# Reordered small loads in layer 1: constants ahead of weight panels, the router's loads and the norm's squares inside the merge stage

## The reference, cut to what matters

```python
y_gdn = gdn_output(o_x, x_z, gdn_norm_g[l])          # rms norm per head, times gdn_norm_g, times silu(z)
y_sgu = sgu_mixer(x_u, x_v, lat_chunks, sgu_ln_g[l], sgu_ln_b[l], sgu_w[l], sgu_b[l])
x = x + mod_x[:, 2][:, None, :] * merge_branches(y_gdn, y_sgu, x_gates, w_branch_a[l], w_branch_b[l], w_out[l])
hx = modulate(rms_norm(x, norm_ffn_g[l]), mod_x[:, 3], mod_x[:, 4])
x = x + mod_x[:, 5][:, None, :] * hier_moe(hx, router_group_w[l], router_group_b[l], router_expert_w[l], ...)
```

## Time and profile before

| | us |
|---|---|
| median of 3 runs | 1783.42 (1783.27 to 1786.96) |
| the profiled execution | 1784.11 |
| its span in the profile | 1782.4 |
| TensorE busy | 1526.9 (86%) |
| VectorE busy | 810.9 (45%) |

### The profile page before, as it was taken

One profiled execution on the slowest core, in us unless ns is written; L12 is line 12 of the kernel. 1 busy time (PEld: TensorE's weight loads), 2 busy tenths in 40 slices (PEclk: granted clock), 3 DMA queues, 4 the chain that ended last, 5 costly groups with the idle time before them and its releaser, 6 DMA issues. The chain is left out here.

```text
span 1782.4 us, 19489 instructions
## 1 busy us (share of the span) xinstructions
PE 1526.9 (86%) x7553; PEld 896.7 (50%) x7553; DVE 810.9 (45%) x1512; ACT 371.3 (21%) x700; POOL 191.1 (11%) x280
## 2 busy tenths in 40 slices
PE   4999968779879989475789876999889899999977
PEld 2877766578634434242334333444444447656563
DVE  2344548444456376541211114266573315675553
ACT  3221245111101100110000001000350224642230
POOL 0000016500000000002000000000250001213330
PEclk9899979777989999677989997999999999999998
DMA  9331002220577766569999993433501222121120
GB/s 347 100 94 48 1 1 58 78 83 10 177 269 270 259 246 231 209 242 410 414 364 368 394 382 123 150 133 106 154 3 69 94 72 71 48 95 47 49 72 24
DMA packets 132298, 283.60 MB, mean 159 GB/s; under 512 B 28744, under 2 KB 39272, under 8 KB 126955
## 3 DMA queue, kind: packets, MB, share of 16 engines
q1 hardware_dynamic: 128608, 266.65, 41.6%
q0 software_dynamic: 3600, 15.73, 2.2%
HBM read 312.77 MB, written 4.19 MB: 178 GB/s over the span
## 5 line engine op out<-in xcount | busy, mean ns | idle before, releaser
L1383 PE MATMUL ps<-ring,hTx 128*128 128x512 f32 x256 | 113.4, 600 | 3.4 <-PEq L176 1.8
L2678 PE MATMUL ps<-hT,ring 128*128 128x512 f32 x256 | 111.8, 593 | 3.1 <-PEq L2585 2.8
L325 DVE SCALAR_TENSOR_TENSOR ada_acc<-ring,cact,ada_acc 128x512 f32<-128x512 f32 x154 | 104.1, 744 | 0.5
L629 PE MATMUL ps<-hTx,ring 128*128 128x256 f32 x384 | 91.0, 392 | 5.3 <-PEq L176 5.3
L2313 PE MATMUL ps<-hT,ring 128*128 128x512 f32 x208 | 90.4, 592 | 0.0
L629 PEld LDWEIGHTS ps<-hTx,ring 128*128 128x128 f32 x384 | 74.7, 197 | 19.6 <-issue 8.0
L1383 PEld LDWEIGHTS ps<-ring,hTx 128*128 128x128 f32 x256 | 48.7, 193 | 62.8 <-issue 60.4
L2678 PEld LDWEIGHTS ps<-hT,ring 128*128 128x128 f32 x256 | 47.9, 190 | 61.0 <-issue 61.0
L1899 PE MATMUL ps<-ring,hTx 128*32 128x512 f32 x384 | 54.0, 713 | 26.8 <-DMA ring<-in_expert_w 26.8
L720 DVE SCALAR_TENSOR_TENSOR conv<-xpad,taps,conv 128x512 f32<-128x512 f32 (+1 forms) x96 | 63.6, 663 | 3.4
L2313 PEld LDWEIGHTS ps<-hT,ring 128*128 128x128 f32 x208 | 39.5, 190 | 48.5 <-issue 48.3
(11 more groups left out here) (526 smaller groups left out, 2723.7 us busy)
## 6 DMA issues: line engine op xcount, KB each, us to landing
ring<-in_expert_w SPq DMA_DIRECT2D x24, 2048.0 KB, 14.7
far<-in_expert_w SPq DMA_DIRECT2D x24, 2048.0 KB, 18.6
ring<-in_w_in SPq DMA_DIRECT2D x16, 2048.0 KB, 12.8
ring<-in_ada_w SPq DMA_DIRECT2D x12, 2048.0 KB, 9.6
ring<-in_w_ada SPq DMA_DIRECT2D x12, 2048.0 KB, 8.9
ring<-in_w_in_c SPq DMA_DIRECT2D x10, 2048.0 KB, 8.4
ring<-in_expert_w POOLq DMA_DIRECT2D x32, 512.0 KB
far<-in_expert_w POOLq DMA_DIRECT2D x32, 512.0 KB
```

Of the source, the lines that this page charges most:

```text
L325: ins = dve.scalar_tensor_tensor(out=part, in0=slot[:, kt], scalar=c[:, kt:kt + 1], in1=part, op0=ALU.mult, op1=ALU.add)
L629: ins = pe.matmul(ps[:, j % BANKS, s * L:(s + 1) * L], slot[:, kt, (j % 4) * P:(j % 4 + 1) * P], (hTc, hTx)[s][:, kt], start=(kt == 0), st ...
L1383: ins = pe.matmul(ps[:, 2 + i % BANKS], hTx[:, kt, t * P:(t + 1) * P], stream.slot(n)[:, kt], start=(kt == 0), stop=(kt == KT - 1))
L2678: ins = pe.matmul(bank, slot[:, kt, j % 4 * P:(j % 4 + 1) * P], hT[:, kt], **edge)
```

## The change

1. In the u/v/gate block SP issues the five small loads `spw`, `spb_row`, two `ln_rows` and `gn_row` before the two panels rather than behind them. The four bias rows `mods` stay behind.
2. SP issues the seven loads that the router needs (`grow`, two parts of `wr`, two of `br`, `slots`, `slot_col`) in the merge block, behind `xs`, `mod_x` and `mod_c`, and ahead of the block's panels. SP waits at the block's end until they have landed; TensorE and VectorE no longer wait for them in the route block. Their tiles move to a scope that lives longer.
3. The two squares of `xs` move from the head of the route block to the end of the merge block on ScalarE; their elementwise output goes to `merged`, which is no longer used by then.
4. In the merge block VectorE waits for the bias rows behind the second `dot`, ahead of the first `put`, rather than ahead of everything.

```diff
@@ u/v/gate block
                     def _(sp):
-                        stream.issue(sp, uvg[1] + 1)
                         sp.dma_start(spw[:, :, :], w["sgu_w"][0].rearrange("g p q -> p g q")).then_inc(loaded, 16)
                         sp.dma_start(spb_row[:, :], w["sgu_b"][0]).then_inc(loaded, 16)
                         sp.dma_start(ln_rows[:, 0], row_bcast(w["sgu_ln_g"][0])).then_inc(loaded, 16)
                         sp.dma_start(ln_rows[:, 1], row_bcast(w["sgu_ln_b"][0])).then_inc(loaded, 16)
                         sp.dma_start(gn_row[:, :], row_bcast(w["gdn_norm_g"][0])).then_inc(loaded, 16)
+                        stream.issue(sp, uvg[1] + 1)
@@ merge block
+                        sp.dma_start(grow[:, :], row_bcast(w["norm_ffn_g"][0])).then_inc(route_loaded, 16)
+                        sp.dma_start(wr[:, :, 0:GROUPS], pkt(w["router_group_w"][0])).then_inc(route_loaded, 16)
+                        sp.dma_start(wr[:, :, GROUPS:], pkt(w["router_expert_w"][0])).then_inc(route_loaded, 16)
+                        sp.dma_start(br[:, 0:GROUPS], row_bcast(w["router_group_b"][0])).then_inc(route_loaded, 16)
+                        sp.dma_start(br[:, GROUPS:], row_bcast(w["router_expert_b"][0])).then_inc(route_loaded, 16)
+                        at, n = parts["slots"]
+                        sp.dma_start(slots[:, :], const_dram[:, at:at + n]).then_inc(route_loaded, 16)
+                        at, n = parts["slot_col"]
+                        sp.dma_start(slot_col[:, :], const_dram[:, at:at + n]).then_inc(route_loaded, 16)
                         stream.issue(sp, ab_in[0])
+                        sp.wait_ge(route_loaded, 112)
...
                     def _(dve):
-                        dve.wait_ge(bias_loaded, 32)
                         for i in range(4 * TT):
                             if i % TT == 0 and i // TT < 3:
                                 dot(dve, i // TT)
+                                if i == TT:
+                                    dve.wait_ge(bias_loaded, 32)
                                 if i:
                                     put(dve, i // TT - 1)
...
+                        for t in range(TT):
+                            act.wait_ge(added, TT + t + 1)
+                            act.activation(merged[:, t], xs[:, t], ACT.Square, accum_out=stat[:, t:t + 1])
@@ route block
-                            sp.dma_start(grow[:, :], row_bcast(w["norm_ffn_g"][0])).then_inc(loaded, 16)
...
-                            for t in range(TT):
-                                if t:
-                                    act.wait_ge(squares, t)
-                                act.activation(sqr[:, :], xs[:, t], ACT.Square, accum_out=stat[:, t:t + 1]).then_inc(squares, 1)
                             act.wait_ge(steps, 1)
...
-                            pe.wait_ge(loaded, 112)
...
-                            dve.wait_ge(squares, TT)
                             dve.tensor_scalar(stat[:, 2:4], stat[:, 0:2], 1.0 / D, EPS, ALU.mult, ALU.add).then_inc(steps, 1)
-                            dve.wait_ge(loaded, 112)
                             dve.scalar_tensor_tensor(out=gm[:, :], in0=mods[:, 2], scalar=1.0, in1=grow[:, :], op0=ALU.add, op1=ALU.mult).then_inc(steps, 1)
```

More of the change, by code:

```diff
@@ L1302, in build @@
             mods = sb(first, "mods", [P, 4, D])
+            grow = sb(first, "grow", [P, D])
+            wr = sb(first, "wr", [P, KT, ROUTER])
+            br = sb(first, "br", [P, ROUTER])
+            slots = sb(first, "slots", [P, SLOTS])
+            slot_col = sb(first, "slot_col", [P, SLOTS // P])
             branches = first.enter_context(ExitStack())
@@ L1489, in build @@
                     ssem(n) for n in ("proj", "gated", "summed", "turned", "moved", "outed", "scaled", "added"))
-                bias_loaded, x_loaded = ssem("bias_loaded"), ssem("x_loaded")
+                bias_loaded, x_loaded, route_loaded = (ssem(n) for n in ("bias_loaded", "x_loaded", "route_loaded"))
                 BANKS = 6
@@ L1628, in build @@
                 with ExitStack() as scope:
-                    grow = sb(scope, "grow", [P, D])
                     gm = sb(scope, "gm2", [P, D])
@@ L1650, in build @@
                     ssem = stage_sems(scope, "route_")
-                    loaded, squares, steps, std, turned, moved, routed, ge_done, e2_done, chain, ordered, chosen_done, ranked, gated, slotted, rowed = (
-                        ssem(n) for n in ("loaded", "squares", "steps", "std", "turned", "moved", "routed", "ge_done", "e2_done", "chain", "ordered", "chosen_done",
+                    steps, std, turned, moved, routed, ge_done, e2_done, chain, ordered, chosen_done, ranked, gated, slotted, rowed = (
+                        ssem(n) for n in ("steps", "std", "turned", "moved", "routed", "ge_done", "e2_done", "chain", "ordered", "chosen_done",
                                           "ranked", "gated", "slotted", "rowed"))
```

13 lines of the change are left out of this document (removed).

## The result

| | before, beside it | changed |
|---|---|---|
| median, us | 1785.18 (1783.27 to 1787.12, 8 runs) | 1774.15 (1770.67 to 1781.40, 8 runs) |
| ratio | | 0.9943, 95% interval 0.9924 to 0.9962 |
| span of the profiled execution | 1782.4 | 1769.9 |

The ratio is a gain of 10.2 us (6.8 to 13.6). It is faster, as forecast, but 1774.15 is 6.7 us above the forecast of 1767.4 and outside its range of 1763.0 to 1771.5. Six microseconds less came than the 16.0 forecast. Of the changed kernel's eight runs four took 1770.7 to 1772.0 us and four 1776.3 to 1781.4, and the median stands between the two groups; the profiled execution, 1772.01, is of the lower one.

What follows compares the result with a forecast made beforehand. TensorE was taken as the bound from 512 to 611.7, with winnable waits before and behind it; gains of 4.0 + 2.0 + 10.0 = 16.0 us gave a span-based 1768.1 and a median of 1767.4 us, range 1763.0 to 1771.5.

Steps and rivals of the forecast that it cites:

- part 2: Merge block: `w_branch_b` issued earlier, its landing set by the queue with seven loads added, 647.4 instead of 649.37; gain 2.0 us.
- starting value of 1783.4: Whole kernel: the profiled execution's 1784.11 us less 0.7 for the median, from which the gains were taken.
- Faster at all: Whole kernel: the claim that the change is faster by over 0.2%; chance 0.95.
- Part 1, gain 4.0: Head of the u/v/gate block: `gn_row` lands early, the third `uvg` panel ends at 519.3 instead of 523.35; gain 4.0 us.
- Part 3, gain 10.0: Head of the route block: first product for `h2` 1.8 us after the block's start instead of 11.8; gain 10.0 us.
- the rival: Merge: `wr` stalls SP and `w_branch_b` lands late; ends slower only if it lands at 667 or later; chance 0.02.
- rival of dearer loads: Merge and u/v/gate: small loads cost more than their share, merge loses 2.5 us; 1770.5 to 1774 us; chance 0.2.
- Clock: Waits for second `uvg` panel and `w_branch_b` end at the lower clock, costing 2.5 us each; rival, clock stays up: chance 0.13.

Runs made afterwards that it cites:

- e11_squares_back: e3_loads_last with the two squares of `xs` back at the head of the route block; 1771.42 us, ratio 0.9901.
- e2_nohead: The changed kernel with the five small loads of the u/v/gate block back in their old order behind the panels; 1777.33 us, ratio 0.9950.
- e5_few_pieces: The changed kernel with `wr` loaded as contiguous rows, 128 pieces per part instead of 1024, and copied into place by GpSimd; 1772.75 us, ratio 0.9915.
- e6_wait_only: The kernel before with only VectorE's wait for the merge's bias rows moved behind the second `dot`; 1774.50 us, ratio 0.9935.
- e12_no_part4: The changed kernel with the wait for the bias rows left at the front of the merge's first `dot`; 1776.15 us, ratio 0.9937.
- e3_loads_last: The changed kernel with the seven router loads issued behind the merge's last panel; 1763.01 us, ratio 0.9868.
- e8_best: e3_loads_last with only `gn_row` ahead of two `uvg` panels, the third ahead of `ln_rows` and `mods`, and the `mods` wait behind the second `dot`; 1761.13 us.
- e4_best: e3_loads_last with `gn_row`, `spw` and `spb_row` ahead of two `uvg` panels, the third panel ahead of `ln_rows` and `mods`; 1766.35 us, ratio 0.9873.
- e10_best_again: The same kernel as e8_best, run again with more runs; 1760.11 us, ratio 0.9837.
- e16_wr_last: The changed kernel with both parts of `wr` and `br` behind the merge's last panel, `grow`, `slots` and `slot_col` left ahead; 1767.83 us, ratio 0.9886.
- e1_head: The kernel before with only the five small u/v/gate loads moved ahead of the two panels; 1781.79 us, ratio 0.9970.
- e7_after_again: The changed kernel, unaltered, measured once more; 1772.99 us, ratio 0.9923.

## Why the prediction was wrong in size and right in sign

The step of the mechanism that failed is the one of part 2 that took SP's stall as harmless and let the queue alone set when `w_branch_b` lands. In size a second step weighs more: that all outside the three blocks stays at nothing, from a starting value of 1783.4. Of the 6.7 us above the forecast 1.8 lie in that starting value (before's median was 1785.18 beside the changed kernel) and 5.0 in the gain, 11.0 us between the medians instead of 16.0; of these, 1.2 are part 2's and most of the rest lies outside the blocks.

- **Faster at all** (0.95): right. The third `uvg` panel is no longer late, and the route block no longer waits for its loads.
- **Part 1, gain 4.0**: measured 4.6, 2.8 and 5.2 (139.8, 141.6 and 139.2 in the three traces of the changed kernel, against before's mean of 144.4). Its steps held: second panel 20.1 us after the block's start (20.4 measured), a wait of 6.1 (6.46), the third panel with time in hand. Counted from the block's start `dot` 0 comes 1.2 us later than forecast (15.0 against 13.8), and the third panel still came in time.
- **Part 3, gain 10.0**: measured 10.3 (46.8 to 36.5 in the means). e11_squares_back puts 2.4 of it on the squares.
- **Part 2, gain 2.0**: this is the step that failed. Measured 0.8 (means of four and three traces), in the trace of e2_nohead nothing. I wrote that the panel is "issued right behind the panel of 625.80" and that "what then sets its landing is the queue". In the changed kernel SP itself sets it. I had seen `spw` and `spb_row` hold SP for 9.4 us, doubled it for the rival ("Two such stalls, 19 us from 613, end at 632, while the queue is still full to 636") and took the end at 632 as harmless. The stall did end near there: 611.75 + 13.06 + 3.88, then 630.20. The fault lies in the second half: the queue is full to 636 before only because the second `w_ada_2` panel is issued at 625.80. Held behind SP, that panel is not in it, and the queue ran dry at 628. So the panel landed 37.7 us into the block instead of 35.7, and the products behind it gave 1.0 us back by a clock that rose sooner (15.51 us instead of the 16.50 kept). That 1774.15 stands at the end of the rival of dearer loads (1770.5 to 1774) is chance: by it the merge block would be 2.5 us longer than before, and it is 0.8 shorter. A stall past a panel's old issue time costs, even if it ends while the old queue was full. e5_few_pieces takes the stall away, fills the hole in the queue and lands the panel at 35.2 us.
- **Clock**: the sum kept 2.5 us for the lower clock in both gaps (16.50 less 14.00 in the merge). Waits of 5.94 and 6.46 us did end at it (15.51 and 15.54 for 32 products, 1.5 us above 14.00), so the lower clock was there and its price too high by 1.0 each time in the profiled execution. The other traces of the changed kernel have 16.54 and 16.00 in the merge.
- **What I did not ask**: what part 4 brings without part 2. The terms have it: without the seven loads `w_branch_b` lands at 641.4, before `total` 0 ends at 642.0, so the products start 7.4 us earlier and 2.5 faster, a gain of 9.9. e6_wait_only shows 10.1 us in the merge for the one moved wait, and e12_no_part4 only 2.0 with the loads ahead. By the same terms the seven loads cost 7.9 us where they stand. Measured they cost 7.4 us between traces that began the block at the lower clock (116.8 against 109.4 in e3_loads_last) and 9.4 between traces that did not (117.2 against 107.8 in e8_best). Part 4 paid for them, and so the block looked unchanged.
- **The rest of the difference**: by means of the traces the three blocks gained 4.2, 0.8 and 10.3, together 15.3 us; the medians show 10.2 (6.8 to 13.6) and 13.8 (9.5 to 18.2). The sum in the blocks was thus nearly as forecast, in part by luck, since the clock's price, set too high, made up for half of the panel's lateness in the profiled execution. Only 1.2 us of the miss belong to the failed step. The other 1.5 to 5 us lie in stretches whose instructions are the same: by means over the same traces the u/v/gate block starts 0.7 us later, expert block and layer 2's head (196.4 before, 197.1 with the change) are 0.7 and 0.6 longer, while single traces of before alone differ there by 5.2, 2.9 and 1.4 us. Whether they belong to the change stays open; for the block's start nothing bears it out.
- **The range** was too narrow: I built it from bounds of terms and left no room for what a second measurement of the same kernel moves (before: medians of 1783.4, 1785.2 and 1787.2).

## What to carry to other kernels

When loads are put ahead of large transfers on one queue, ask twice: how many bytes they put in front, and until when they hold the engine that issues everything behind them; in this kernel a stall would have been harmless only if it had ended before the next large transfer could be issued. Look for the waits that stand further forward than their data is used: moving one of them gave 10 us in its block here, with nothing added to the queue, and a load put late gives nothing back while its wait stays at the front (e4_best). Put the loads that a block needs at its head behind the last large transfer of the block ahead: e3_loads_last did so and ran at a ratio of 0.9868 (0.9853 to 0.9883), which beats both kernels. With `gn_row` alone in front besides, e10_best_again ran at 1760.11 us, ratio 0.9837 (0.9808 to 0.9865); what that adds shows in the u/v/gate block (134.9 and 135.6 us, against 139.2 to 142.0 with part 1's order) and not yet in the whole time.

## What the runs showed of the hardware that I had not expected

- One load of 128 KiB in 1024 pieces behind full panels held SP's issue for 13.0 us in all five traces that have it there (12.99 to 13.06). It stands right behind another load of 1024 pieces, of 16 bytes each, whose own issue took 0.82 to 1.37 us. Behind the merge's last panel the same load held SP for 3.7 to 4.8 us (six traces), and 1.30 us at the head of the route block of e6_wait_only, with an empty queue. In contiguous rows it took 0.64 us behind the same panels. What fills up and holds SP, no run here shows.
- Short waits also ended at the lower clock, of 1.2 GHz, where the forecast knew only 4.70 us and more: 1.88 us (15.70 for 32 products in e16_wr_last), 2.14 (15.70), 2.81 (15.56) and 3.36 (16.83), while 0.90 to 1.55 us did not (14.00 each). They cost 1.6 to 2.8 us. The length of the wait alone does not decide. Behind the barrier at the merge block's head TensorE was idle for 1.83 to 1.93 us in every trace, and the same 64 products took 28.07 us in some (before, e1_head, e7_after_again, e8_best) and 29.64 to 29.77 in others (the changed kernel, e3_loads_last, e12_no_part4, e16_wr_last). The row of e7_after_again, a second trace of the changed kernel, to be held against 29.67 above:

```profile
611.33 28.07 PE L1526 MATMUL ps<-ring,ygT 128*128 128x512 f32 x64 [1.83 <-PEq L176]
```

- The time of one program goes with the mean granted clock of its run. Of 17 runs of before beside one group, those with a clock of 0.915 to 0.917 took 1782.7 to 1786.3 us, those with 0.908 to 0.910 took 1787.2 to 1792.5. A kernel with fewer waits also had the higher clock: 0.9182 in the mean over e10_best_again's six runs, 0.912 over before's.
